# Loading the gate weights of the convolution layer into the expert buffer, in four pairs of blocks

## The reference, cut to what matters

```python
h = x @ w_pw1 + b_pw1                       # 1024 -> 2048
u = h[..., :D_MODEL] * jax.nn.sigmoid(h[..., D_MODEL:])
ext = jnp.concatenate([past, u], axis=1)    # past: 30 state rows per sample sequence
conv = depthwise(ext, w_dw) + b_dw          # width 31, 1024 channels
z = layer_norm(conv, g_cn, b_cn)
z = z * jax.nn.sigmoid(z)
return z @ w_pw2 + b_pw2, ext[:, -30:]
```

## Time and profile before

| | |
|---|---|
| median of 3 runs | 1187.49 us (1184.72 to 1192.29) |
| the profiled execution | 1192.26 us, of which its span is 1190.6 us |
| PE busy | 1006.8 us, 85% of the span |
| DVE, ACT, POOL busy | 35%, 15%, 9% |
| chain that ended last | PE 73%, DVE 11%, DMA 6% |
| PE's granted clock, mean | 0.908 of full speed |

### The profile page before, as it was taken

The page is one execution under the profiler, slowest core; times in us unless marked ns, Lnnn a source line. Parts: engine busy times, 40 slices in busy tenths (PEclk is TensorE's granted clock), DMA queues, the critical chain, the costliest instruction groups (busy, mean ns, idle before and its releaser), DMA issues.

```text
span 1190.6 us, 14515 instructions
## 1 busy us (share of the span) xinstructions
PE 1006.8 (85%) x4808; PEld 501.1 (42%) x4809; DVE 411.1 (35%) x902; ACT 174.5 (15%) x333; POOL 101.6 (9%) x190
## 2 busy tenths in 40 slices
PE   3989898999989999849989785589798899999993
PEld 3656445533323333326646543344563233333331
DVE  2545445232232323361134322211521432332336
ACT  1000223111001110111123222111211011111000
POOL 2050000100000000023000002200010000000000
PEclk9999997699989999979889897799769899999998
DMA  7584524998769999938030102219637469999981
GB/s 208 156 265 111 191 101 143 379 374 297 252 216 350 379 379 386 368 99 277 14 141 1 40 23 67 88 64 360 236 123 243 158 226 374 379 380 378 383 306 45
DMA packets 131447, 266.68 MB, mean 224 GB/s; under 512 B 7338, under 2 KB 39110, under 8 KB 131379
## 3 DMA queue, kind: packets, MB, share of 16 engines
q1 hardware_dynamic: 121184, 237.75, 56.5%
q10 hardware_dynamic: 4979, 16.15, 3.9%
q0 software_dynamic: 5232, 12.08, 3.8%
HBM read 259.52 MB, written 7.15 MB: 224 GB/s over the span
## 4 chain that ended last, share of the span: by engine, by line
PE 73%; DVE 11%; DMA 6%; issue 4%; SPq 3%; ACT 3%; ACTq 0%; DVEq 0%
PE bank L942 11%; PE bank L934 11%; PE wide L934 9%; PE bank L974 4%; PE bank L872 4%; PE bank L760 3%; PE wide L872 2%; PE bank L1041 2%; PE wide L760 2%; PE bank L1693 2%; DMA w<-in_e_w 2%; PE bank L776 2%; DMA w<-in_state_conv 2%; DMA dbuf<-in_a_w_pw 2%; PE bank L1594 2%
## 5 line engine op out<-in xcount | busy, mean ns | idle before, releaser
L942 PE MATMUL bank<-w,dbuf 128*64 128x512 f32 x512 | 135.5, 677 | 18.3 <-DVE dbuf L1352 17.0
L934 PE MATMUL bank<-w,dbuf 128*64 128x512 f32 x512 | 118.0, 611 | 4.5 <-issue 1.4
L934 PE MATMUL wide<-w,dbuf 128*64 128x512 f32 x512 | 113.4, 595 | 0.0
L1357 DVE COPY dbuf<-bank 64x512 f32<-64x512 f32 x64 | 44.1, 689 | 138.5 <-PE bank L942 138.0
L974 PE MATMUL bank<-dbuf,ukT 128*128 128x512 f32 (+1 forms) x144 | 79.3, 654 | 12.7 <-DVE dbuf L1367 5.9
L942 PEld LDWEIGHTS bank<-w,dbuf 128*64 128x64 f32 x512 | 45.2, 152 | 84.8 <-issue 84.5
L934 PEld LDWEIGHTS bank<-w,dbuf 128*64 128x64 f32 x512 | 41.7, 141 | 76.5 <-issue 74.7
L1693 PE MATMUL bank<-ident,w 128*128 128x128 f32 (+1 forms) x192 | 34.0, 335 | 34.8 <-DMA w<-in_cache_ckv 26.5
L934 PEld LDWEIGHTS wide<-w,dbuf 128*64 128x64 f32 x512 | 35.4, 137 | 65.0 <-issue 63.9
L529 POOL COPY idx_col<-idx 64x1 int32 (+1 forms) x30 | 5.3, 177 | 611.1 <-PE bank L921 421.1
L516 POOL DMA_DIRECT2D w<-in_cache_kpe x64 | 34.3, 536 | 267.4 <-PE bank L1748 164.4
(11 more groups left out here) (341 smaller groups left out, 1325.9 us busy)
## 6 DMA issues: line engine op xcount, KB each, us to landing
w<-in_e_w SPq DMA_DIRECT2D x90, 2048.0 KB, 16.2
dbuf<-in_a_w_pw SPq DMA_DIRECT2D x16, 512.0 KB, 5.8
w<-in_cache_ckv SPq DMA_DIRECT2D x64, 128.0 KB, 2.2
w<-u_rows SPq DMA_DIRECT2D x32, 142.0 KB, 2.9
dbuf<-in_a_w_pw ACTq DMA_DIRECT2D x1, 4096.0 KB, 17.1
dbuf<-in_e_w SPq DMA_DIRECT2D x2, 2048.0 KB
dbuf<-in_b_w_o SPq DMA_DIRECT2D x1, 4096.0 KB, 14.1
x_tok<-in_e_w SPq DMA_DIRECT2D x2, 1536.0 KB, 11.5
```

Of the source, the lines that this page charges most:

```text
L934: last = nc.tensor.matmul(bank[n * C:(n + 1) * C], x[:, k], w[n][k], start=(k == 0), stop=(k == KD - 1))
L942: last = nc.tensor.matmul(bank[n * C:(n + 1) * C], h[:, k], w[k][:, n * 512:(n + 1) * 512], start=(k == 0), stop=(k == 3))
L1357: last = V.tensor_copy(y_pair[s * C:(s + 1) * C, h * 512:(h + 1) * 512], B[4 + s][h * C:(h + 1) * C, :])
```

## The change

`w_pw1` is cut in four pairs of blocks (2 MB each, two transfers with 1024 bytes per row). Each pair has a place of its own: the first in `dbuf`, the others in `w13[0]` and `w2[0]`, which hold no expert yet. SP waits for x and the parameters, loads the first pair, waits until it has landed, and loads the other three and `w_pw2` in a row. x is now loaded by ACT, the parameters by SP. `replicate` moves from SP to POOL, behind the scaling of x, which no longer waits for three gated blocks but for POOL's own loads, the zeroing of `x_rows` among them. The state is turned by PE after `gated(0)` and copied by DVE after `glu(0)`. The weights of expert 0 are loaded when all eight blocks are gated. ACT's copy of the state to the output moves from j = 2 to j = 6. Some semaphores are merged: `ld_q` into `ld_kv`, `own_ready` into `ld_uv`, `trash_set` into `ld_misc`, `ld_ident` into `ld_x[0]`.

```diff
-        pw1 = [part(dbuf, s * 2048, KD, 2, P) for s in range(2)]
+        pw1 = [part(*v, KD, 2, 2 * P) for v in ((dbuf, 0), (w13[0], 0), (w13[0], 4096), (w2[0], 0))]
...
         def sp_program(sp):
-            sp.dma_start(ident[:], a["c_ident"]).then_inc(ld_ident, 16)
-            for n, (t0, m) in enumerate(TILES):
-                src = a["x_prompt"][0, t0:t0 + m] if n < 2 else a["x_sample"].rearrange("b s d -> (b s) d")
-                sp.dma_start(x_tok[0:m, n], src).then_inc(ld_x[n], 16)
+            sp.dma_start(ident[:], a["c_ident"]).then_inc(ld_x[0], 16)
+            sp.dma_start(dw_rows[0:CW], a["a_w_dw"][0]).then_inc(ld_vec, 16)
+            for j, (name, n) in enumerate(VECS):
+                r0 = sum(c for _, c in VECS[:j])
+                sp.dma_start(vec_rows[r0:r0 + n], a[name][0].rearrange("(r c) -> r c", c=P)).then_inc(ld_vec, 16)
             w1v = a["a_w_pw1"][0].rearrange("(k p) (h c) -> p k h c", p=P, h=2)
-            for s in range(2):
-                load_pw1(s, s)
-            sp.wait_ge(glu_done, 2)
-            for j in range(KD):
-                if j + 2 < KD:
-                    sp.wait_ge(h_done, j + 1)
-                    load_pw1(j + 2, j % 2)
-                replicate(j)
+            for i in range(3):
+                sp.wait_ge(ld_x[i], 32 if i == 0 else 16)
+            sp.wait_ge(ld_vec, 16 * (len(VECS) + 1))
+            for q in range(4):
+                if q == 1:
+                    sp.wait_ge(pw1_ready[0], 32)
                 for h in range(2):
+                    sp.dma_start(pw1[q][:, :, h], w1v[:, :, h, bass.ts(q, 2 * P)]).then_inc(pw1_ready[q], 16)
+            sp.dma_start(pw2, a["a_w_pw2"][0].rearrange("(k p) n -> p k n", p=P)).then_inc(pw2_ready, 16)
...
+            sp.wait_ge(h_done, KD)
             load_13(0, 0, 0)
             load_2(0, 0, 0)
...
         def pool_program(pool):
...
             pool.wait_ge(xT_turned, 6)
-            pool.wait_ge(glu_done, 6)
             pool.wait_ge(ld_misc, MISC)
...
+            for j in range(KD):
+                replicate(j)
...
         def act_program(act):
+            for n, (t0, m) in enumerate(TILES):
+                src = a["x_prompt"][0, t0:t0 + m] if n < 2 else a["x_sample"].rearrange("b s d -> (b s) d")
+                act.dma_start(x_tok[0:m, n], src).then_inc(ld_x[n], 16)
...
                 gate_half(j)
-                if j == 2:
-                    act.dma_start(pw2, a["a_w_pw2"][0].rearrange("(k p) n -> p k n", p=P)).then_inc(pw2_ready, 16)
+                if j == 6:
                     act.dma_start(a["conv_sample"][0, :, 0:CS - DS], a["state_conv"][0, :, DS:CS])\
                         .then_inc(out_stored, 16)
                 if j >= 4:
                     square(j - 4)
...
         def pe_program(pe):
             gated(0)
+            turn_state()
             gated(1)
...
         def dve_program(dve):
             for j in range(KD):
                 glu(j)
+                if j == 0:
+                    copy_state()
                 samples(j)
```

More of the change, by code:

```diff
@@ L99, in trunk_step @@
     NVEC = sum(n for _, n in VECS)
-    MISC = 9 * 16
+    MISC = (9 + DEPTH) * 16
     SHIFTS, GROUPS, STEPS = 4, 4, 8
@@ L374, in replicate @@
[L374 to L383, removed]
-                    sp.dma_start(copies[j % 2][32 * d:32 * d + 32],
-                                 u_rows[j % 2][:, d:d + WC].rearrange("(g c) x -> c g x", g=GROUPS))\
-                        .then_inc(copied[j % 2], 16)
@@ L449, in sp_program @@
             sp.wait_ge(mix_done, 3)
-            sp.wait_ge(trash_set, 16 * DEPTH)
+            sp.wait_ge(ld_misc, MISC)
             sp.wait_ge(u_stored, 32)
@@ L487, in pool_program, with replicate @@
                 pool.dma_start(rows[T:ROWS].rearrange("r (h c) -> r h c", h=4),
-                               zeros[0:C].unsqueeze(1).to_broadcast([C, 4, SEQ])).then_inc(trash_set, 16)
+                               zeros[0:C].unsqueeze(1).to_broadcast([C, 4, SEQ])).then_inc(ld_misc, 16)
+            def replicate(j):
+                pool.wait_ge(glu_p, j + 1)
+                if j == 0:
+                    pool.wait_ge(state_set, 1)
+                if j >= 2:
+                    pool.wait_ge(copied[j % 2], j // 2 * 16 * SHIFTS)
+                pool.dma_start(u_rows[j % 2], ext[:, j, 0:WC + 4]).then_inc(bounced[j % 2], 16)
+                pool.wait_ge(bounced[j % 2], (j // 2 + 1) * 16)
+                if j >= 2:
+                    pool.wait_ge(conv_done, j - 1)
+                for d in range(SHIFTS):
+                    pool.dma_start(copies[j % 2][32 * d:32 * d + 32],
+                                   u_rows[j % 2][:, d:d + WC].rearrange("(g c) x -> c g x", g=GROUPS))\
+                        .then_inc(copied[j % 2], 16)
             pool.wait_ge(xT_turned, 6)
-            pool.wait_ge(glu_done, 6)
             pool.wait_ge(ld_misc, MISC)
@@ L739, in pe_program, with turn_state @@
             last.then_inc(par_turned, 1)
-            pe.wait_ge(ld_state, 32)
-            for h in range(2):
-                for q in range(2):
-                    for k in range(4):
-                        last = nc.tensor.transpose(B[4 + 2 * h + q][:, k * 4 * CS:(k + 1) * 4 * CS],
-                                                   state[0:4 * CS, h, (4 * q + k) * P:(4 * q + k + 1) * P],
-                                                   ident[0:4 * CS, 0:4 * CS])
-                    last.then_inc(par_turned, 1)
+            def turn_state():
+                pe.wait_ge(ld_state, 32)
+                for h in range(2):
+                    for q in range(2):
+                        for k in range(4):
+                            last = nc.tensor.transpose(B[4 + 2 * h + q][:, k * 4 * CS:(k + 1) * 4 * CS],
+                                                       state[0:4 * CS, h, (4 * q + k) * P:(4 * q + k + 1) * P],
+                                                       ident[0:4 * CS, 0:4 * CS])
+                        last.then_inc(par_turned, 1)
             pe.wait_ge(xT_copied, 6)
@@ L759, in gated @@
                     for k in range(KD):
-                        last = nc.tensor.matmul(B[2 * s + h][:, 0:T], pw1[s][:, k, h], xT[:, k], start=(k == 0),
-                                                stop=(k == KD - 1))
+                        last = nc.tensor.matmul(B[2 * s + h][:, 0:T], pw1[j // 2][:, k, h, s * P:(s + 1) * P], xT[:, k],
+                                                start=(k == 0), stop=(k == KD - 1))
                 last.then_inc(h_done, 1)
```

73 lines of the change are left out of this document (34 added, 39 removed).

## The result

| | before | changed |
|---|---|---|
| median of 4 runs each | 1188.99 us (1184.72 to 1192.29) | 1206.78 us (1201.16 to 1211.5) |
| ratio | | 1.0142, 95% interval 1.0108 to 1.0176 |
| the profiled execution | 1192.26 us, span 1190.6 us | 1202.54 us, span 1200.9 us |

I had forecast 1189.1 us in a range of 1179 to 1199.

The account below looks back on a forecast made before the run. PE, busy for 85% of the span, was taken as the bound, with waits and slow stretches to be had. -6.3 + 2.7 + 0.9 + 4.3 = +1.6 us on the median of 1187.49 gave 1189.1 us, range 1179 to 1199.

Parts of the forecast that it names:

- The middle: Around `conv(1)` and `gated(4)`: PE's stop of 4.3 us and the slow block's 1.9 us go, -6.3 us.
- The start: Up to `gated(1)`: parameters at 18.5, first pair 8.5 us, then the state's turn of 3.44 us; +2.7 us.
- It is the crowd that delays them: At the start: the 0.15 MB of parameters land at 20.8 because of the other transfers; with gate weights removed, 18.5.
- The first pair: Before `gated(0)`: the first 2.1 MB of gate weights take 8.5 us to load, bounds 6.0 and 10 us.
- Gaps ahead of `gated(0)` cost no clock today; I take the same: At the start: PE's wait leaves the granted clock at 1.00, so the first block takes 8.62 us.
- POOL's queue at `conv(0)`: `replicate(0)` on POOL's queue beside the weights: mostly hidden, nothing or up to 5 us if copies take twice as long.
- the third rival: `replicate` on POOL's queue paces the convolutions, about +6 at `conv(0)`, +10 at `conv(7)`, slow clock +2: +15, 1203 us; chance 0.1.
- DVE's work draws them out: Before the first `replicate`: POOL's 17.4 us of x scaling, if drawn out by DVE's work, still has 3 us of cover.
- ACT at j = 6: The state's copy to the output, 0.85 us to issue, goes on the path ahead of `square(2)`: +0.9 us.
- The last block: Before `conv(7)`: `replicate(7)` runs under expert 0's weights and its copies land late; +4.3 us, ends 0 and 10.
- The first rival: Last block not late, the software queue being as quick in a crowd as the hardware one: -2.7, 1184.8 us; chance 0.2.
- The second: At the start: parameters land early, at 12 to 14; start -3, sum -4 to -8, 1181 with the last block's stop; chance 0.2.

Follow-up runs that it names:

- two pairs of runs: Expert 0's weights issued early against late: changed kernel 1.0142 against 1.004; kernel before with `replicate` on POOL 1.016 against 1.0054.
- `w_pw2` late: Kernel before with the 31 rows in two loads, `w_pw2` and the state's copy to the output issued behind `square(2)` at j = 6: 1178.94 us, 0.9911.
- second series: The changed kernel measured once more, nothing edited, 6 runs: 1203.94 us, 1.0121 of the kernel before.
- expert 0 late: Changed kernel with expert 0's weights issued only after the last copies of `replicate` have landed: 1192.37 us, 1.004 of the kernel before.
- state first: Changed kernel with the state's transposes put back ahead of `gated(0)`: 1204.16 us, 1.0123 of the kernel before.
- paced: Changed kernel: 16 + 15 rows, expert 0's weights and x scaling late, 50 transposes before `gated(0)`, state and later weights held back, output copy at j = 2: 0.9917.
- two right edits: Changed kernel with the state turned ahead of `gated(0)`, 1204.16 us; or with 40 transposes keeping PE at work before `gated(0)`, 1207.22 us (one execution).

## Why the prediction was wrong, step by step

- **The middle, -6.3: right.** -6.0 measured. Stop and slow block both went.
- **The start, +2.7: measured +6.6.** By its terms: parameters +3.3, pair and hops -0.6, cold block +3.1, state -1.8, in all +4.0 on 2.7. The parameters were to land at 18.5 and came at 21.77. "It is the crowd that delays them" was wrong: it was the 31-row transfer, as the two runs with 16 + 15 rows show. I had the rule before me and took it for 1 us at most; I had taken the x tile's 9.7 and the crowd's bytes for evidence. The first pair, 8.5, was right (8.4 from its first issue), in part by luck: the 377 GB/s that I took for 2 KB rows come from a window whose packets average 5.3 KB (3.23 MB in 614 packets). "Gaps ahead of `gated(0)` cost no clock today; I take the same" was wrong: the window whose clock I read held no matmul to show it, and in the kernel before the state's transposes, the first work after the wait, took the slow stretch on themselves. Two windows of the changed kernel (columns: length; busy us of PE, PEld, DVE, ACT, POOL; then granted clock, DMA share, GB/s), the first 4 us of the slow `gated(0)`, and of the slow `conv(7)`:

```profile
30.00:34.00 4.00, 3.58 (x7) 2.41 (x8) 3.97 (x2) 0.00 (x0) 4.00 (x3) 1.00 0.62 196
...
147.00:151.00 4.00, 3.29 (x32) 1.80 (x36) 0.00 (x0) 0.00 (x0) 0.00 (x0) 0.50 1.01 399
```

  In the first, 7 matmuls take 3.58 us, 0.51 each, half the speed of `gated(1)`'s 8.62 / 32 = 0.27, yet the clock reads 1.00; in the second it reads 0.50. And the state's turn cost 1.64 us, not 3.44, since the 3.44 of rows 1, twice that for the same 16 transposes, had followed a wait of 3 us.
- **POOL's queue at `conv(0)`, "nothing, or up to 5": 1.5.** Within the bounds; the landing, 7.7 us, was near the point of 8 that the third rival named. The wait stayed hidden behind a late, slow `gated(0)`: as soon as `gated(1)` comes 2.6 to 3.4 us earlier it becomes 3.2 to 3.4 us, and with a `conv(0)` of 5.35 takes back the whole gain. "DVE's work draws them out" I had the wrong way round: POOL's work drew out DVE's.
- **ACT at j = 6, +0.9: +0.5.** The wait for `square(2)` grew from 0.44 to 0.94.
- **The last block, +4.3: +8.9, the largest error.** That the early stream makes `replicate(7)` late was right, as two pairs of runs show. The step that failed is its price: two trips at 5.6 and 6 us, read off 32 KB loads, and nothing for the slow block. Against the forecast's steps `u_rows(7)` left 0.3 us later, took 0.7 more, and the copies 1.6 more (8.1 to the last landing, not 6): a stop of 6.6 for 4.1 (my own steps add up to 142.7, not 142.5). And the slow `conv(7)`, put at "at most 1.9" and left out of the sum, took 2.3 more. In every run with this stop, of 6.0 to 8.7 us, the block after it took 4.92 to 6.60 us instead of 3.59. I also laid the delay on POOL's software queue ("0, if the software queue is no slower than the hardware one in a crowd"). The trace of the run with `w_pw2` late does not bear that out: SP's hardware queue needed 8.4 and 5.3 to 7.9 us for the same two trips under a stream. The step that makes the last block late is the early issue of expert 0's weights, not the move of `replicate`.
- **Rivals.** The third, with its place at `conv(7)`, its price there of 10 and the slow clock after, was the nearest: 1203 against 1206.78. Its nearness is partly luck: it had 6 us at `conv(0)`, where 1.5 were measured, and the measured median holds some 6 us that no trace accounts for. I gave it 0.1, since 142 KB seemed small beside 256 KB gathers. The first rival's premise, a software queue as quick in a crowd as the hardware one, holds as far as the runs show, but the last block was late all the same, because in a crowd both are slow. The second's 1181 doesn't follow from its terms: -6.3 - 3 + 0.9 + 4.3 = -4.1 gives 1183.4. The point I set for it, a landing of 8 us for the copies, was just reached at `conv(7)` (8.1) and nearly at `conv(0)` (7.7).

**What stays open.** From the start of the matmuls behind the norm on, the two profiled executions differ by -1.3 us, the sum of the terms being 11.5 and the span's difference 10.3; but the medians differ by 17.8 us. In the second series they differ by 15.7, with a module that is 13.1 longer. Most of the other kernels' medians follow their module to within 4 us, as this second series does (expert 0 late +2.0 and +1.4, state first +12.8 and +13.2, `w_pw2` late -10.5 and -9.6; but paced -6.5 and -11.9). One source of such scatter can be seen. PE's clock in the attention does not take the same course in every profile, and what decides it is not known: windows of the kernel before, then of the run with expert 0 late:

```profile
616.70:636.70 20.00, 16.73 (x58) 11.22 (x57) 7.78 (x31) 6.01 (x20) 0.00 (x0) 0.74 0.29 117
```

```profile
616.80:636.80 20.00, 16.54 (x81) 11.69 (x81) 9.09 (x38) 7.03 (x24) 0.00 (x0) 1.00 0.27 111
```

From PE's first matmuls of the attention (536.68 in rows 12) to the first scores against the cache (L1715, at 683.61) it takes 146.9 us in the one case, 139.8 in the other. A third course, with 0.83 in this window, takes 142.3; three of the profiles have it. Both profiles of the changed kernel have the slow course, but so has that of the kernel before. Whether the changed kernel falls into it more often would need many profiles of each, and was not settled. So 6 us of its first median and 3 of its second are unexplained.

## What to carry to other kernels

A stream of megabytes issued just ahead of a small round trip through DRAM made each trip of it 4 to 7 us longer here, on the software queue and on the hardware queue alike; count the trips, add the cold block behind the stop, and put the stream behind the last trip unless someone waits for it. Before pricing a late small load by the bytes around it, look at its outermost size: 31 rows as 16 + 15, alone on the kernel before, gained 0.4%, where the whole rearrangement lost 1.4%. And a gain early in a chain must be followed to the next meeting point, here `conv(0)`, whose own path, DVE and two DMA trips, took back the whole gain, about 3 us, of either of two right edits.

## What the runs showed of the hardware that I had not expected

- One transfer of 31 rows (124 KB) landed at 20.8 and 21.8 us, as 16 + 15 rows at 11.4 and 11.9. With the two loads, the later tiles of x came sooner in the changed kernel, and the state in the kernel before.
- 16 DVE copies of 32x64 took 3.75 us alone, 15.00 beside POOL's operations on 128x1024; one of them 5.0 us.
- The granted clock reads 1.00 in the first 4 us of `gated(0)`, where matmuls run at half speed; after the stop at `conv(7)` it reads 0.50. The length of a known block is the surer sign.
- 142 to 144 KB through the software queue at the last block: 2.0 to 3.1 us in calm, 6.5 to 8.1 under expert 0's weights (rows of 2 and 4 KB; DMA share 0.95 and 1.05, 332 and 319 GB/s while the two trips ran), and up to 9.4 in the second profile. Through the hardware queue: 1.7 to 3.3 in calm, 5.3 to 8.4 under `w_pw2`.
